# Block 2's attention: two constant matmuls ahead of a unit's scores where a unit has no value sums

## The reference, cut to what matters

```python
def joint_dense_attention(q, k, v, kc, vc):
    ...
    kk = jnp.concatenate([kc, k], axis=1)
    vv = jnp.concatenate([vc, v], axis=1)
    ...
    def block(qi):
        sc = jnp.einsum('bqkgd,bnkd->bkgqn', qi, kk, preferred_element_type=jnp.float32) * (d ** -0.5)
        p = jax.nn.softmax(sc, axis=-1)
        return jnp.einsum('bkgqn,bnkd->bqkgd', p.astype(vv.dtype), vv)
```

## Time and profile before

| | us |
|---|---|
| median of 2 runs | 2559.28 (2556.6 and 2561.96) |
| profiled execution | 2565.05 |
| its span, first to last instruction | 2563.9 |
| TensorE busy | 2404.0 (94% of the span), 10725 matmul instructions |
| DVE busy | 898.4 (35%) |
| ACT busy | 542.1 (21%) |
| mean granted TensorE clock | 0.968 of full speed |

### The profile page before, as it was taken

The page is one execution under the profiler, slowest core; times in us unless marked ns, Lnnn a source line. Parts: engine busy times, 40 slices in busy tenths (PEclk is TensorE's granted clock), DMA queues, the critical chain, the costliest instruction groups (busy, mean ns, idle before and its releaser), DMA issues. The chain is left out here.

```text
span 2563.9 us, 28249 instructions
## 1 busy us (share of the span) xinstructions
PE 2404.0 (94%) x10725; PEld 1169.0 (46%) x10725; DVE 898.4 (35%) x2080; ACT 542.1 (21%) x1279; POOL 220.8 (9%) x391
## 2 busy tenths in 40 slices
PE   6999999969999899999999988999998789999999
PEld 2655676543343333333333333756444444454443
DVE  2354554242121111121112113533565763342472
ACT  2244431110000000000000002211454552211350
POOL 1000442020101001000101002000000000000000
PEclk9999999979999999999999998999899999999999
DMA  9201597358999999999999999120000002112000
GB/s 345 90 33 66 204 313 291 142 221 349 425 426 427 412 414 384 411 428 400 387 426 410 427 427 364 49 95 33 1 1 1 1 1 91 50 67 98 0 34 33
DMA packets 122659, 562.47 MB, mean 219 GB/s; under 512 B 19033, under 2 KB 43038, under 8 KB 94738
## 3 DMA queue, kind: packets, MB, share of 16 engines
q1 hardware_dynamic: 104600, 517.55, 50.3%
q0 software_dynamic: 15024, 37.87, 4.0%
q10 hardware_dynamic: 2890, 5.13, 0.6%
HBM read 534.16 MB, written 26.35 MB: 219 GB/s over the span
## 5 line engine op out<-in xcount | busy, mean ns | idle before, releaser
L234 PE MATMUL ps<-ring,mem 128*128 128x512 f32 (+5 forms) x1136 | 383.0, 493 | 8.6 <-ACT mem L3095 3.6
L1960 PE MATMUL ps<-ring,mem 128*32 128x512 f32 (+2 forms) x1632 | 365.5, 603 | 11.0 <-issue 11.0
L234 PE MATMUL ps<-mem,ring 128*128 128x512 f32 (+1 forms) x928 | 365.5, 553 | 0.0
L234 PEld LDWEIGHTS ps<-ring,mem 128*128 128x128 f32 x1136 | 196.3, 192 | 176.6 <-issue 152.3
L234 PEld LDWEIGHTS ps<-mem,ring 128*128 128x128 f32 x928 | 175.7, 191 | 176.0 <-issue 171.0
L1960 PE MATMUL ps<-mem 128*32 128x512 f32 (+2 forms) x800 | 221.6, 614 | 5.8 <-issue 5.8
L240 PE MATMUL ps<-mem 128*128 128x128 f32 (+2 forms) x1157 | 189.3, 296 | 37.8 <-PEq L2406 10.7
L1960 PEld LDWEIGHTS ps<-ring,mem 128*32 128x32 f32 (+2 forms) x1632 | 123.0, 133 | 215.5 <-issue 213.2
L240 PEld LDWEIGHTS ps<-mem 128*128 128x128 f32 (+2 forms) x1157 | 146.3, 165 | 159.2 <-issue 115.8
L2055 DVE TENSOR_SCALAR mem<-ps,mem 128x128 f32<-128x128 f32 x168 | 57.4, 405 | 319.4 <-PE ps L240 319.4
L2016 PE MATMUL ps<-ring,mem 128*32 128x512 f32 (+2 forms) x848 | 161.6, 593 | 6.8 <-issue 6.8
(11 more groups left out here) (390 smaller groups left out, 2550.3 us busy)
## 6 DMA issues: line engine op xcount, KB each, us to landing
ring<-in_w_up SPq DMA_DIRECT2D x72, 2048.0 KB, 20.2
ring<-in_w_down SPq DMA_DIRECT2D x44, 2048.0 KB, 24.1
mem<-in_w_up SPq DMA_DIRECT2D x40, 2048.0 KB, 22.1
mem<-in_w_down SPq DMA_DIRECT2D x20, 2048.0 KB, 27.5
ring<-in_w_ada SPq DMA_DIRECT2D x12, 2048.0 KB, 7.5
mem<-in_w_up SPq DMA_DIRECT2D x40, 512.0 KB, 11.3
ring<-in_mod_w SPq DMA_DIRECT2D x8, 2048.0 KB, 12.7
ring<-in_w_up SPq DMA_DIRECT2D x24, 512.0 KB, 20.7
```

The source lines that it names most:

```text
L234: i = e.matmul(o, l, r, start=(start and n == 0), stop=(stop and n == len(pairs) - 1))
L1960: m = e.matmul(PS[n][c0:c0 + rows, :], XGT[:, u, k * 128 + c0:k * 128 + c0 + rows], wt[:, kk, n * 512:n * 512 + 512], start=False, stop=(k ...
```

## The change

In the loop of `pe_attention`, iterations from 1 on whose list of value sums is empty first issue two matmuls of constants: the 128x128 block of ones with the 256 columns of `cst0`, once into the left and once into the right half of bank 6. Each starts and stops its own accumulation, and nothing reads the result. `sums_done` counts the value sums that TensorE has finished; once there is one, the block first waits until DVE has multiplied out that many (`values_taken`), since it writes the bank where they were. No other engine's program changes.

```diff
         score(0)
+        sums_done = 0
         for x in range(len(units)):
             if x + 1 < len(units):
+                if x and not A.sums[x]:
+                    if sums_done:
+                        e.wait_ge(*taken_.at(sums_done))
+                    for c in range(2):
+                        e.matmul(PS[6][:, 256 * c:256 * c + 256], ones, cst0, start=True, stop=True)
                 score(x + 1)
+            sums_done += sum(1 for g, j, *_ in A.sums[x] if j == len(A.groups[g][2]) - 1)
             steps(filler, rate)
             values(A.sums[x])
             if x:
```

## The result

The changed kernel takes 2600.15 us (2598.66 and 2601.65) against 2559.28: ratio 1.0166, 95% interval 1.0136 to 1.0195, slower by 1.7%. The forecast was 2602 us.

The account below looks back on a forecast made before the run. TensorE was taken to set the pace in GQA, MLA-1 and window, DVE in MLA-0; +14.5, +2.0, +14.2 and +11.9 make +42.6 us on 2565.05, so 2607.7, or 2602 from the runs' median; own range 2590 to 2612.

Parts of the forecast that it names:

- The number and the price of blocks: 76 blocks over the four attention stages, each costing 0.86 to 1.06 us at full clock, taken as 0.95.
- the 2.9 to 3.1: Sign that the forecast is right: MLA-1's unit goes from 2.00 us to 2.9 to 3.1.
- 0.6 and 0.35 for blocks in 256-column units: Partly hidden blocks: four in GQA cost 0.6 us each, two in MLA-1 cost 0.35 each.
- The stages where TensorE sets the pace: GQA, MLA-1 and the window stage: a unit begins where the one before ends, so most blocks are exposed.
- Rival C: Blocks hide in the slack of the ring from score to transposes; at 0.2 us a block 2557 us; chance 0.06.
- The waits: Blocks right after a finished sum wait for DVE's multiply at nine places, 1.81 us at worst, 7.7 in all.
- The clock: Blocks were expected to hold it in GQA, returning 15.5 us there and 5.2 in MLA-0.
- The reason given: GQA's clock holds through 128-row matmuls in every unit without value sums and idle time before the exponential partly filled.
- Rival A: The clock falls all the same: 20.7 us stay lost, some nine blocks run at half clock, 2631 us; chance 0.22.
- 27.1: Cost in us of GQA's 32 blocks: two free, four at 0.6, the other 26 exposed at 0.95.
- the 2%: About what a measurement of this kernel can tell from none, 51 us; chance 0.66 of staying within it.

## Why the prediction was right

2602 forecast, 2600.15 measured, and by the mechanism that was named: the blocks cost more than the clock they win back. The closeness is luck in part. The stages were forecast to grow by 42.6 us and grew by 37.2 in the traces, and the two medians of two runs each happen to lie 40.9 apart. Point by point:

- *The number and the price of blocks.* 0.95 was taken between 0.86 and 1.06. A block adds 0.86 in GQA and 0.82 in MLA-1 where no wait lasts; where one does, its start to the score's is 0.1 longer (1.06 for 0.96 in GQA and the window stage). The lower bound was nearer, since the weights of a block do load under the transposes: in MLA-1's unit its first weight load starts at 2106.59, and the last transpose started at the same time. So MLA-1's unit came to 2.82, below the 2.9 to 3.1 that was to show the forecast right. It was also wrong to charge 0.6 and 0.35 for blocks in 256-column units: there the idle time of the unit behind took them up whole. These two are most of what MLA-1 was cheaper than forecast (+10.7 for +14.2). The window stage (+9.1 for +11.9) pays 10.8 against its 109.8 us at full clock in the kernels with blocks at the idle time; the other 1.7 are its slow clock of before, which was put at nothing to win.
- *The stages where TensorE sets the pace* were the right ones. Rival C (0.2 us a block) is refuted by the unit lengths, and by the kernel without blocks in MLA-1 and the window stage.
- *The waits.* 7.7 us forecast from DVE's rows of before, 7.3 measured, the worst at 1.80 us where 1.81 stood. What was missed is that a long wait is idle time as any other and can drop the clock. In the changed kernel that is 6.8 us at half clock, some 3 us. With the blocks gone the waits and the clock together are 16 us, of which the clock's share varies with the execution.
- *The clock.* It was expected to hold and mostly did: slow time in GQA and MLA-0 fell from 54.6 to 17.0 us. Its worth was misjudged in both directions: 15.5 taken for GQA where 12.7 is all there was in that execution, 5.2 for MLA-0 of 7.3. The reason given, matmuls over 128 rows in every unit and the idle time partly filled, was right in its second half for the first stretch, where one block in the idle time did what eight had done. For the second place both may be needed.
- *Rival A* (0.22) did not come. Part of it did: 10.2 us stay in GQA.

So the sum: against a GQA at full clock (157.4 us) the changed kernel pays 26.7 us for its 32 blocks, of which 2.8 are waits and up to 5 the slow time left; against the 12.7 us that it wins. Its blocks alone thus cost 19 to 24 us, where 27.1 stood. In the two last stages it pays 21.5, 10.7 and 10.8, against 1.7 of slow clock that there was.

Errors of opposite sign cancelled in part, then: blocks priced too high on one side; on the other the waits' effect on the clock left out, and a clock gain in GQA taken 3 us too large. In GQA they cancelled nearly whole (+14.0 for +14.5); in MLA-1 and the window stage nothing stood against the price. And a slowdown of 1.7% was told from none with an interval of 1.4 to 2.0%, so the 2% that the prediction took for the least that can be told was too much.

## What to carry to other kernels

Before work is added to hold the clock, read where the clock falls and what TensorE did just before: here it was mostly behind idle time of 1.4 to 2.2 us in otherwise full stretches, and matmuls placed in that idle time cost nothing that the traces show and won 0.5%, while the same matmuls in every unit cost 1.7%. Count filler at its full rate wherever units begin back to back. And a filler that needs a wait of its own may bring the very idle time that it is to remove; put it where its wait is long over. Since the same program has more slow time in one execution than in the next, lay a slow stretch to a cause only when it comes and goes with it over several.

## What the runs showed of the hardware that was not expected

- A wait of 1.72 us by TensorE, in a stage that otherwise keeps it full, was followed by 17.1 us at half clock with TensorE busy for 16.97 of them. The idle time is a tenth of what follows. It does not always follow: over all profiles with the two long waits, 1.8 us in GQA and 1.7 in the window stage, the clock fell behind 9 of 13.
- Matmuls over 64 rows run beside matmuls over the other 64 rows: 2.30 us for a unit with the block and 2.29 without. The Trainium skill (TensorE: Matmul & The Clock Gate, "The mechanism") says that tiles of different row groups overlap, and the trace agrees.
- Over the same rows, or beside operands of 96 rows, 64 rows are no cheaper than 128 and can be dearer: 0.97 us from a block's start to the score's in GQA against 0.96, and 3.21 us a unit of MLA-1 against 2.82.
